# First attention of a two-block network: its output product cut into pieces between the attention units

## What is computed

```python
def window_gqa(hx, hc, wq, wk, wv, wo, sink, cos, sin, need_ctx):
    q = apply_rope((hx @ wq).reshape(B, L, A_KV_HEADS, G, HEAD_DIM), cos, sin)
    ...
        s_lat = jnp.where(valid, s_lat, NEG_INF)          # own block and its two neighbours
        s_ctx = jnp.einsum('bqhgd,bchd->bhgqc', qblk, kc).astype(jnp.float32) * scale
        p = softmax_with_sink(jnp.concatenate([s_lat, s_ctx], axis=-1), sink_f).astype(v.dtype)
        o = jnp.einsum('bhgqk,bkhd->bqhgd', p[..., :3 * BLOCK], vblk)
        return o + jnp.einsum('bhgqc,bchd->bqhgd', p[..., 3 * BLOCK:], vc)
    ...
    out_x = jnp.moveaxis(ob, 0, 1).reshape(B, L, A_HEADS_2 * HEAD_DIM) @ wo
# and in the block
        ax, ac = window_gqa(...)
        x = layer_norm(alpha * x + g1 * ax, ln1_g[i], ln1_b[i])
        fx = sqrelu_mlp(x * (1.0 + sc2) + sh2, mlp_w1[i], mlp_w2[i])
```

## Time and profile before

| | |
|---|---|
| median of 3 runs | 2836.56 us (2830.61 to 2842.97) |
| profiled execution, its own time | 2834.9 us |
| its span (first to last instruction) | 2831.5 us |
| mean granted clock of PE | 0.97 of full speed |
| attention units, first scores to last values | 1151.1 to 1346.9 us |
| output product | 1350.0 to 1419.6 us |

### The profile page before, as it was taken

The page is one execution under the profiler, slowest core; times in us unless marked ns, Lnnn a source line. Parts: engine busy times, 40 slices in busy tenths (PEclk is TensorE's granted clock), DMA queues, the critical chain, the costliest instruction groups (busy, mean ns, idle before and its releaser), DMA issues.

```text
span 2831.5 us, 38915 instructions
## 1 busy us (share of the span) xinstructions
PE 2658.7 (94%) x14540; PEld 2142.0 (76%) x14540; DVE 1265.7 (45%) x1888; ACT 654.1 (23%) x1223; POOL 1331.5 (47%) x862
## 2 busy tenths in 40 slices
PE   7989999989999989899989999999879998899997
PEld 6667777767777768666868888888668886778886
DVE  6941222262222254444364444444666554455545
ACT  2221000041000023566031000000445553211112
POOL 6356555535555553233445443333253311676661
PEclk9999999999999999899989999999999998999998
DMA  5124444434444432000111111111101110222231
GB/s 187 48 83 153 145 148 148 149 112 139 146 148 148 148 105 67 16 1 1 53 38 60 59 59 59 59 62 63 39 30 44 44 36 16 82 90 96 96 96 52
DMA packets 67367, 235.54 MB, mean 83 GB/s; under 512 B 8144, under 2 KB 9552, under 8 KB 67152
## 3 DMA queue, kind: packets, MB, share of 16 engines
q1 hardware_dynamic: 65792, 233.64, 25.3%
q10 hardware_dynamic: 1488, 0.69, 0.1%
HBM read 232.21 MB, written 2.10 MB: 83 GB/s over the span
## 4 chain that ended last, share of the span: by engine, by line
PE 86%; DVE 5%; issue 4%; ACT 2%; POOL 1%; DMA 1%; DVEq 0%; SPq 0%; ACTq 0%; POOLq 0%
PE ps L593 67%; PE ps L1091 2%; PE ps L786 2%; PE ps L748 2%; PE ps L990 2%; PE ps L1063 1%; PE ps L976 1%; PE ps L1113 1%; DVE X L1964 1%; PE ps L712 1%; PE ps L636 1%; DMA raw<-in_stream 1%; PE ps L944 1%; PE ps L951 1%; ACT arena L1149 1%
## 5 line engine op out<-in xcount | busy, mean ns | idle before, releaser
L464 POOL TENSOR_SCALAR whi<-raw 128x1024 fp32r<-128x1024 f32 x332 | 365.4, 1101 | 1174.3 <-DMA raw<-in_stream 1174.2
L466 POOL TENSOR_TENSOR wlo<-raw,whi 128x1024 fp32r<-128x1024 f32 x332 | 808.7, 2436 | 27.7
L593 PE MATMUL ps<-Ahi,whi 128*128 128x512 f32 (+1 forms) x2128 | 729.7, 374 | 36.7 <-DVE Alo L1581 17.7
L593 PE MATMUL ps<-Alo,whi 128*128 128x512 f32 (+1 forms) x2128 | 721.4, 370 | 0.0
L593 PE MATMUL ps<-Ahi,wlo 128*128 128x512 f32 (+1 forms) x2128 | 719.9, 369 | 0.0
L593 PEld LDWEIGHTS ps<-Ahi,whi 128*128 128x128 f32 x2128 | 376.0, 190 | 129.1 <-issue 21.5
L593 PEld LDWEIGHTS ps<-Ahi,wlo 128*128 128x128 f32 x2128 | 375.8, 190 | 69.3
L593 PEld LDWEIGHTS ps<-Alo,whi 128*128 128x128 f32 x2128 | 376.6, 191 | 66.7 <-issue 0.7
L593 PE MATMUL ps<-hhi,whi 128*128 128x512 f32 x1120 | 373.3, 370 | 19.7 <-DVE X L1964 18.7
L593 PE MATMUL ps<-hhi,wlo 128*128 128x512 f32 x1120 | 373.4, 370 | 0.0
L593 PE MATMUL ps<-hlo,whi 128*128 128x512 f32 x1120 | 370.7, 368 | 0.0
(11 more groups left out here) (267 smaller groups left out, 2808.3 us busy)
## 6 DMA issues: line engine op xcount, KB each, us to landing
raw<-in_stream SPq DMA_DIRECT2D x428, 512.0 KB, 3.7
X<-in_xT SPq DMA_DIRECT2D x2, 1024.0 KB, 6.7
arena<-in_dft SPq DMA_DIRECT2D x1, 2048.0 KB, 17.4
out_xT<-X SPq DMA_DIRECT2D x2, 1024.0 KB, 4.3
X<-in_ctxT SPq DMA_DIRECT2D x1, 1024.0 KB, 19.7
w<-in_stream SPq DMA_DIRECT2D x2, 512.0 KB, 4.3
vec<-in_vec SPq DMA_DIRECT2D x1, 364.5 KB, 7.8
arena<-in_fmap SPq DMA_DIRECT2D x1, 256.0 KB, 12.8
```

The source lines that it names most:

```text
L464: pool.tensor_scalar(whi[:, s, part], raw[:, s, part], 1.0, 1.0, ALU.mult, ALU.mult).then_inc(sem("w_hi"), 1)
L466: pool.tensor_tensor(wlo[:, s, part], raw[:, s, part], whi[:, s, part], ALU.subtract).then_inc(sem("w_split"), 1)
L593: mm = pe.matmul(dst[c], w[:, b % RING, off:off + P], rhs(k, part, c0, n), start=(k == 0 and w is whi and part == 0), stop=(k == kn - 1 an ...
```

## The change

The product is cut into 64 pieces `(p, m, c)`: a pair p of `O` tiles (two tiles of 128 features), an output tile m, and c for the columns of x or of the context. A piece is six matmuls over the two tiles of its pair. From unit 33 on, PE runs one piece at the end of two units out of three (`FILLED`; 46 of the 64 pieces), and the other 18 after the units: two of pair 2 and all sixteen of pair 3. Each piece is added to X at once, by DVE at the start of its next unit. The pieces of pairs 0 to 2 share PSUM bank 7, for which the turned probabilities give up their second place: they now use bank 4 (and bank 5 for the fifth tile) in every unit. ACT copies the high half of a pair behind unit 32, 56 or 80, and DVE subtracts behind 33, 57 or 81, right ahead of the pair's first piece. The pairs' halves lie in tiles of `Alo` and `kd`. SP loads the weights of the product by pairs (rows of 512 features), and POOL splits pairs 1 to 3 in steps between units. The reciprocal now stands ahead of `take_query` on DVE, and `modulations(1)` stands in the query products before the units.

```diff
+PIECES = [(p, m, c) for p in range(4) for m in range(KT) for c in range(2)]
+FILL_FIRST = 33
+FILLED = {FILL_FIRST + 3 * (i // 2) + 2 * (i % 2): i for i in range(48)}
+PAIR_HI = {24 * p + 32: p for p in range(3)}
+PAIR_LO = {24 * p + 33: p for p in range(3)}
+PAIR_SPLITS = {1: (4, 6, 8, 10, 12, 14), 2: (18, 20, 22, 24, 26, 28), 3: (66, 68, 70, 72, 74, 76)}
...
+        def pair_split(p, kk):
+            return (Alo[:, 6 + kk, :], kd_r[:, kk, :]) if p % 2 else (Alo[:, 2 + kk, :], Alo[:, 4 + kk, :])
+        def piece_bank(i):
+            p, m, c = PIECES[i]
+            return 7 if p < 3 else 2 * (m % 4) + c
...
             for u in range(N_UNITS):
+                for p, units in PAIR_SPLITS.items():
+                    if u in units:
+                        pair_weights(p, units.index(u))
                 pool.wait_ge(*when("denA", u + 1))
...
             def turned(u, t):
-                at = (4 + u % 2) * 512 + t * P if t < 4 else 7 * 512
+                at = 4 * 512 + t * P if t < 4 else 5 * 512
                 return psf[:, at:at + P]
...
                 pe.wait_ge(*when("pA", u + 1))
-                pe.wait_ge(*when("ptA", u + 1))
+                pe.wait_ge(*when("ptA", u + 2))
                 for t in range(len(ks)):
-                    if t == 4:
-                        pe.wait_ge(*when("ptA", u + 2))
...
+            def out_piece(i):
+                p, m, c = PIECES[i]
+                b, (c0, n) = B_WOA + p, X_CTX[c]
+                if m % 4 == 0 and c == 0:
+                    pe.wait_ge(*when("w_split", SPLITS[b] + m // 4 + 1))
+                if m == 0 and c == 0:
+                    pe.wait_ge(*when("OA_split", 2 * p + 2))
+                before = i if p < 3 or i < 56 else i - 7
+                if i > 0:
+                    pe.wait_ge(*when("woA_evac", min(before, 48) if p == 3 and i < 56 else before))
+                for kk in range(2):
+                    hi, lo = pair_split(p, kk)
+                    at = m // 2 * 512 + kk * 256 + m % 2 * P
+                    for w, o in ((whi, hi), (whi, lo), (wlo, hi)):
+                        mm = pe.matmul(ps[:, piece_bank(i), 0:n], w[:, b % RING, at:at + P], o[:, c0:c0 + n],
+                                       start=(kk == 0 and w is whi and o is hi), stop=(kk == 1 and w is wlo))
+                mm.then_inc(sem("w_used" if m % 4 == 3 and c else "woA_done"), 1)
...
-            dense("woA", B_WOA, X_CTX, "OA_split")
-            pe.wait_ge(*when("woA_evac", 5))
-            layernorm("l1", X_CTX, "woA_evac", 0)
+                if u in FILLED:
+                    out_piece(FILLED[u])
+            for i in range(max(FILLED[u] for u in FILLED if u < N_UNITS + LEAD + 3) + 1, len(PIECES)):
+                out_piece(i)
+            pe.wait_ge(*when("woA_evac", 48 + 10))
+            layernorm("l1", X_CTX, "woA_evac", 48, 2)
...
+            def pair_hi(p):
+                act.wait_ge(*when("oA", 6 * p + 7))
+                if p >= 2:
+                    act.wait_ge(*block_used(B_WOA + p - 2))
+                for kk in range(2):
+                    copy(pair_split(p, kk)[0], O[:, 2 * p + kk, :]).then_inc(sem("OA_hi"), 1)
...
+            def pair_lo(p):
+                for kk in range(2):
+                    dve.wait_ge(*when("OA_hi", 2 * p + kk + 1))
+                    hi, lo = pair_split(p, kk)
+                    dve.tensor_tensor(lo, O[:, 2 * p + kk, :], hi, ALU.subtract).then_inc(sem("OA_split"), 1)
...
             for u in range(N_UNITS + LEAD + 4):
+                if u - 1 in FILLED and u - 1 < N_UNITS + LEAD + 3:
+                    add_piece(FILLED[u - 1])
...
                     dve.tensor_reduce(sm[:, u % 8, 0:1], psf[:, a:a + W + 1], AX_X, ALU.max, negate=True).then_inc(sem("nmA"), 1)
-                    if u in TAKE_AT:
-                        take_query(*TAKE_AT[u])
-                    if u == KEYS_AT:
-                        take_keys(1)
                 if 1 <= u < N_UNITS + 1:
                     c = sm[:, (u - 1) % 8, :]
                     dve.wait_ge(*when("sA_free", u + 2))
                     dve.reciprocal(c[:, 2:3], c[:, 1:2]).then_inc(sem("denA"), 1)
+                if u in TAKE_AT:
+                    take_query(*TAKE_AT[u])
+                if u == KEYS_AT:
+                    take_keys(1)
...
+                if u in PAIR_LO:
+                    pair_lo(PAIR_LO[u])
+            pair_lo(3)
+            for i in range(FILLED[max(u for u in FILLED if u < N_UNITS + LEAD + 3)] + 1, len(PIECES)):
+                add_piece(i)
```

More of the change, by code:

```diff
@@ L1397, in take_turned @@
                 nk = len(keys(n))
-                four = (4 + u % 2) * 512
+                four = 4 * 512
                 act.wait_ge(*when("turnA", u + 5))
@@ L1401, in take_turned @@
                 if nk > 4:
[L1402 removed]
+                    copy(ptA[u // 4 % 2][:, 4, h * P:(h + 1) * P], psf[:, 5 * 512:5 * 512 + P])
                     nk = 4
@@ L1422, in _ @@
                         take_keys(1)
-            for k in range(KT):
-                if k == 0:
-                    act.wait_ge(*when("oA", 25))
-                copy(Ahi[:, k, :], O[:, k, :]).then_inc(sem("OA_hi"), 1)
+                if u in PAIR_HI:
+                    pair_hi(PAIR_HI[u])
+            pair_hi(3)
             layernorm("l1", X_CTX, 1)
@@ L1889, in _ @@
                         take_query(0, 0, h)
+                if j == 4:
+                    modulations(1)
             for h in (2, 3):
```

74 lines of the change are left out of this document (51 added, 23 removed).

## The result

Over 11 runs of each kernel, side by side, the median went from 2835.54 us (2830.61 to 2842.97) to 2848.96 us (2835.78 to 2857.18). The ratio is 1.0039, 95% interval 1.0026 to 1.0052: 11 us slower (7.4 to 14.7), a real loss, and inside the half per cent that was called no change. The ratios of this document leave out one run, of e12_query_before, that took 3348.95 us at a granted clock of 0.74.

What follows compares the result with a forecast made beforehand. PE was taken as the bound, busy 94% of the span, so only its idle time or low clock could gain. Terms summed to +8.2 us on the profiled 2834.9, giving 2843.1; with the median 1.7 higher, 2845 us, range 2828 to 2860.

Steps and rivals of the forecast that it cites:

- the four terms for waits: First handover, Second and third, Pieces waiting for an addition, End of the units: +6.7, +5.6, +3.0, +1.0 us.
- First handover: Pair 0 at unit 33: PE's piece 0 waits for both subtractions of the pair, +6.7 us.
- Second and third: Handovers of pairs 1 and 2 at units 57 and 81: PE waits 2.8 us each, +5.6 us.
- Pieces waiting for an addition: Pieces 0 to 47 share one bank, each waiting for DVE's addition of the last: +3.0 us (0 to 6).
- End of the units: After the units, pieces 47 and 48 wait for DVE's subtractions and additions: 4.0 us idle, against 3.1 before, +1.0 us.
- Single place: In every unit, the first transpose waits for ACT's copy of turned probabilities of the unit before: +0.7 us.
- Reciprocals: Units 15 to 32: reciprocals ahead of the query's subtraction recover part of PE's 4.0 us wait for POOL, -1.5 us.
- Filling: From unit 33 on, pieces fill all of PE's idle time among the units: -11.5 us (-8.3 to -14.5).
- Clock: Behind the pause at unit 33, PE runs at 1.2 GHz for a time: +4.2 us (half of 3.4 to 11).
- More idle time than the waits show: Rival: by the share of weight loads, 31 us in the units could be filled, not 11.5; 2825 us, chance 0.17.
- Clock stays low: Rival: low clock costs 11 us behind unit 33, 1.7 at each other handover; +18.4, 2855 us, chance 0.18.
- Subtractions at the slow rate: Rival: pair subtractions in three handovers take 1.73 us each, not 0.95; +4.7, so 2849 us, chance 0.15.

Runs made afterwards that it cites:

- e12_query_before: Kernel before the change, with each query's subtraction one unit later on DVE, behind the next unit's maximum and reciprocal: 2825.37 us, ratio 0.9960 to the kernel before.
- e10_lo: Changed kernel with the pair's two DVE subtractions ahead of the query's in unit 33: 2841.73 us, ratio 1.0019 to the kernel before.
- e9_hi: Changed kernel with ACT's copies of each pair two units earlier, DVE's subtractions left in place: 2845.36 us, ratio 1.0036 to the kernel before.
- e2_early: Changed kernel with each pair's ACT copies and DVE subtractions two units earlier: 2832.60 us, ratio 0.9987 to the kernel before.
- e6_bank: Kernel before the change, with only the one place for turned probabilities (banks 4 and 5 in every unit): 2837.03 us, ratio 0.9999 to the kernel before.
- e3_recback: Changed kernel with only the reciprocal put back behind the query's subtraction on DVE: 2849.49 us, ratio 1.0043 to the kernel before.
- e1_rec: Kernel before the change, with only the reciprocal moved ahead of the query's subtraction on DVE: 2834.64 us, ratio 0.9991 to the kernel before.
- e8_values: e7_both with the move of values ahead of the query in DVE's code, which gave the same program: 2824.60 us, ratio 0.9952 to the kernel before.
- e7_both: Changed kernel with e2_early's edit, piece 47 in bank 5, and pieces 48 to 52 not waiting for its addition: 2826.20 us, ratio 0.9959 to the kernel before.
- e5_warm: Changed kernel with useless matmuls in the handover pauses ahead of pieces 0, 16 and 32: 2840.15 us, ratio 1.0019 to the kernel before.
- e11_query: e8_values with each query's subtraction one unit later on DVE, behind the next unit's maximum, reciprocal and move of values: 2816.15 us, ratio 0.9937 to the kernel before.

## Why the prediction held, and where its terms were off

The forecast was 2845 us, +8.2 on the profiled basis and inside the half per cent; the ratio says +11 (7.4 to 14.7). The mechanism was the forecast's: handovers on PE's path, and low clock behind them. The total is nearer than its terms: the four terms for waits were 3.2 us too high together, the clock was too low, and that these errors pull against each other is luck. By its steps:

- **First handover, +6.7:** 6.40. The chain was as written, in its order. ACT's two copies took 1.56 and not 1.50, DVE's two subtractions 1.83, the whole pause as worked out to 0.3 us. e10_lo and e9_hi show the parts: 3.2 for the query, 1.4 for the copies.
- **Second and third, +5.6:** 4.8. The forecast strung the first copy and two subtractions in a row. What stood ahead of the subtractions was unit 57's maximum and reciprocal (to 1288.0, PE idle since 1287.5), and the two subtractions made the rest; e9_hi shows it: with the copies long done nothing changed.
- **Pieces waiting for an addition, +3.0:** 1.7, once, ahead of unit 66's piece and behind unit 65's query. At units 36 and 38, where I also looked for it, PE did not wait: at unit 36 it came to the piece 0.15 us after the addition had ended. e2_early, whose handovers are gone, has more of it (5.5 us with the end of the units, where the kernel after has 5.1).
- **End of the units, +1.0:** three pauses of 3.3 us where one of 3.1 was, +0.2. I had priced the pair's first subtraction at 1.73; the two took 1.83 together. The last sixteen pieces took 18.96 us (1412.13 to 1431.09), not 17 to 18, because 4.4 us of them ran at half clock.
- **Single place, +0.7:** nothing that can be told (e6_bank, -0.3 us by the ratio).
- **Reciprocals, -1.5:** -1.1 by e3_recback for all units, inside the scatter. Its reason fits the waits: what else is queued behind the subtraction keeps the gain small. e1_rec shows it in the kernel before, where 8.9 of 10.7 us were passed on.
- **Filling, -11.5:** the profile gives 11.8. Pieces 0 to 40 lie ahead of unit 95's scores: 21 x 1.45 + 20 x 0.72 = 44.9 us. 175.74 - 44.9 = 130.9; less the pauses 6.4 + 4.8 + 1.7 = 12.9, and less half of the 15.5 us in which PE was busy at half clock (7.7), leaves 110.3, where it was 122.06.
- **Clock, +4.2:** the term that was too small. In this execution half of the busy time at half clock is 7.7 behind the handovers and 3.0 at the end, less 1.7 at the end before, with 1.7 more just ahead of unit 33: 10.7 us, close to the upper bound of 11. The last 1.7 are chance, as they stand behind the pause of 1.1 us after which e8_values' clock fell and e7_both's did not. On the median e5_warm gives 5.7, uncertain by some 5, for what stands behind the handovers. I had given low clock to the first handover alone; pauses of 2.4 us, too, were each followed by 3.4 us of it. And the 4.2 for the first was right by luck (half of 8.65 is 4.3), for two errors in it cancel. I expected low clock as long as at the first scores, some 22 us, and it was 10.3. And I read its cost from units 0 to 11 and 48 to 59 as from the same work, where the earlier trace rows has 89 matmuls in the one and 130 in the other; the later units turn and multiply by values for a full pipeline. The two executions of those 89 above give the price instead: about 9 us more at half clock (granted 0.53 against 0.67) made them 3.6 us longer, so 22 us of it cost nearer 9 than 4.2 (an estimate from these rows).

With these the parts sum to 12.9 + 0.2 - 11.8 + 10.7 = 12.0 of the 13.6 us that the profiles differ by. The filling is what remains of its own stretch, so this tests the rest alone. The missing 1.6 us lie behind unit 95's scores, where 42.8 us stand against 84.5 - 44.9 = 39.6 and only 0.2 + 1.3 of the difference is explained; they stay open.

**The rivals.** *More idle time than the waits show*, 31 us: no. In e11_query PE waits for nearly nothing, and unit 33 to 95 less its pieces takes 153.59 - 44.9 = 108.7 us: 13.4 less than before. This is between the two sums of waits, 8.3 and 14.5, near the upper. The loads are busy 119.25 / 153.59 = 78% there and not 86%, with almost no wait left, though pieces like the product's make up 44.9 us of it. Whether the loads' remaining idle time could still be had, no run shows. The Trainium skill (Trainium Kernel Development and Optimization, Performance Expectations) takes the busy share of weight loads as a measure of the distance to the roofline; used as I did in the rival, with the product's share as the target for the units, it promised 31 us where 13.4 came.

*Clock stays low*, +18.4, 2855: not on the median, but it names the right term. The truth lay between it and the forecast.

*Subtractions at the slow rate*: no, DVE took 0.95 us for each. But POOL paid. In the second handover, and likewise in the third:

```profile
1287.96 1.81 DVE L1999 TENSOR_TENSOR kd_r<-arena,Alo 128x768 fp32r<-128x768 f32 x2
1288.14 2.11 POOL L626 TENSOR_SCALAR tmp<-tmp,sm 128x512 f32<-128x512 f32 x1 [1.27 <-DVE sm L2023]
```

POOL's scaling of 128x512, 0.69 us elsewhere, lasted 2.11 and ended 0.5 us behind the second subtraction. The other way round, in e12_query_before, POOL scaled from 1215.67 to 1216.36 and a query's subtraction began in that time:

```profile
1215.77 1.40 DVE L1880 TENSOR_TENSOR q<-arena,q 64x768 fp32r<-64x768 f32 x1 [0.19 <-ACT q L1149]
```

It took 1.40 instead of 0.95 us. The Trainium skill says (SBUF — State Buffer, "SBUF: two separate sides") that the one that starts first keeps the port for its whole instruction, and the other is blocked. Both rows agree with it. My reason, that POOL has run out of work, held at the first handover alone, where its last scaling ended at 1218.5 and the pair's first subtraction began at 1221.6; at the other two it was wrong, and the price fell on POOL, where PE did not wait for it.

**Why the change lost.** The filling worked as planned, 11.8 us. It was paid for with three handovers on the path, 11.2 us, and the low clock that they left behind. e2_early takes both away by moving two numbers, and the change then no longer loses: 0.9987 (0.9975 to 0.9999), and 0.9959 and 0.9952 in the two runs of the program with the end repaired too. The last obstacle was a subtraction on DVE that waited for ACT (e11_query, 0.9937).

## What to carry to other kernels

When work is moved between the units of a pipelined loop, look at where its inputs are handed over: an input made in the unit that needs it stops the engine in order, and one made two units earlier cost nothing here. Price a new pause of TensorE with the low clock behind it as well: here every one of 2.4 us and more inside the units was followed by it, and shorter ones some of the time. And when an in-order engine waits for another in the middle of its queue, move the waiting instruction itself back until its input is there (11 us in the kernel before), not the one instruction behind it that shows up in the list of waits (2.6 us, not clear of none).

## What the hardware showed that I had not expected

- The length of a stretch at half clock varies between executions of one program. The first twelve units, which no kernel here changes much, took from 19.2 to 22.9 us over fourteen profiles; one program had 19.16 and 22.78, and behind the same pause of 1.1 us its clock stayed once and fell once. The scatter of single runs (2830.6 to 2843.0 for the kernel before) goes with the clock: of its 23 runs beside e12_query_before, the 13 with a granted clock of 0.970 and more have a median of 2832.1 us and the other ten 2838.7. This makes differences of 3 us between two profiles worth nothing unless the clock of both is looked at.
- The half clock of the handovers lasted 3.4, 6.8 and 10.3 us for pauses of 2.4, 3.2 and 6.4 us, but the length of a pause alone doesn't fix it. The pause of 3.1 us ahead of the output product was followed by 3.4 us of half clock in the kernel before, by 6.8 us in e1_rec and by none in e12_query_before; one of 1.75 us by 3.4 us in e8_values and by none in e7_both.
- Useless matmuls in three pauses were worth 5.7 us (uncertain by some 5) though they let no piece start earlier.
- A GpSimd operation was stretched to three times its length, 0.69 to 2.11 us, by two VectorE subtractions in a row: it ended only behind both.
